# A small bias table in DRAM read as overlapping rows, and a second one spread out in 16 pieces

## The reference, cut to what matters

```python
dist = pos_b[None, :, None] - idx
bias = jnp.moveaxis(rel_bias[t5_bucket(dist)], -1, 2)      # first block: 32 buckets x 16 heads
...
drow = rs + jnp.arange(win_r) - r + WIN_ROWS - 1
bias = jnp.transpose(rpb[:, drow][:, :, dcol], (0, 2, 3, 1, 4))   # second block: 8 heads x 15 x 31
```

## Time and profile before

| | us |
|---|---|
| median of 3 runs | 914.88 |
| lowest and highest | 914.59, 915.59 |
| the profiled execution, its own time | 912.87 |
| span of the profile | 911.1 |

### The profile page before, as it was taken

How to read it: one execution, slowest core, us unless ns; L and a number is a source line. 1 busy time by engine, 2 the same in 40 slices (tenths; PEclk the granted TensorE clock), 3 DMA queues, 4 the chain that set the end, 5 groups by cost and what they waited for, 6 DMA issues and landing times.

```text
span 911.1 us, 17577 instructions
## 1 busy us (share of the span) xinstructions
PE 893.8 (98%) x7192; PEld 869.4 (95%) x7192; DVE 656.3 (72%) x1261; ACT 499.7 (55%) x907; POOL 46.6 (5%) x62
## 2 busy tenths in 40 slices
PE   8999987999999999999999999999999999999998
PEld 7988987999999898899999999999999999999998
DVE  6878626988877695575667555566798788887873
ACT  5695827774435556667768444434545454445551
POOL 0000000000000125200000000021020000000000
PEclk9999997999999999999999999999999999999999
DMA  9918799978877743048545655526445222465541
GB/s 307 313 47 279 142 185 355 305 252 277 293 252 232 246 137 126 2 149 264 181 148 194 205 169 185 189 78 177 161 150 184 93 71 70 140 208 164 180 144 47
DMA packets 164753, 166.30 MB, mean 183 GB/s; under 512 B 16672, under 2 KB 161216, under 8 KB 164416
## 3 DMA queue, kind: packets, MB, share of 16 engines
q1 hardware_dynamic: 164672, 165.17, 57.7%
HBM read 162.01 MB, written 4.98 MB: 183 GB/s over the span
## 4 chain that ended last, share of the span: by engine, by line
PE 83%; DMA 5%; DVE 4%; ACT 3%; SPq 3%; issue 2%; POOL 0%; DVEq 0%; ACTq 0%
PE ps L304 21%; PE ps L306 21%; PE ps L308 21%; DMA e_scratch<-eb 3%; PE ps L1505 2%; PE ps L1503 2%; PE ps L1507 2%; PE ps L1562 2%; PE ps L1076 1%; DVE wl L271 1%; PE ps L1597 1%; PE ps L1599 1%; PE ps L1601 1%; SPq L2174 1%; DMA raw<-in_rec_w_in_dram 1%
## 5 line engine op out<-in xcount | busy, mean ns | idle before, releaser
L304 PE MATMUL ps<-xh,wh 128*128 128x256 f32 x1136 | 326.9, 288 | 8.9 <-ACT tmp L798 8.9
L271 DVE TENSOR_TENSOR wl<-raw,wh 128x1024 fp32r<-128x1024 f32 x256 | 308.5, 1221 | 31.7 <-ACT wh L264 31.5
L306 PE MATMUL ps<-xl,wh 128*128 128x256 f32 x1136 | 322.2, 284 | 0.0
L308 PE MATMUL ps<-xh,wl 128*128 128x256 f32 x1136 | 322.1, 284 | 0.0
L264 ACT ACTIVATE wh<-raw 128x1024 fp32r<-128x1024 f32 x256 | 266.5, 1050 | 94.0 <-PE ps L308 69.2
L304 PEld LDWEIGHTS ps<-xh,wh 128*128 128x128 f32 x1136 | 218.4, 192 | 12.0 <-ACT tmp L798 9.1
L306 PEld LDWEIGHTS ps<-xl,wh 128*128 128x128 f32 x1136 | 218.5, 192 | 0.3
L308 PEld LDWEIGHTS ps<-xh,wl 128*128 128x128 f32 x1136 | 218.4, 192 | 0.0
L304 PE MATMUL ps<-hh,wh 128*128 128x256 f32 x512 | 143.2, 280 | 0.0
L306 PE MATMUL ps<-hl,wh 128*128 128x256 f32 x512 | 143.2, 280 | 0.0
L308 PE MATMUL ps<-hh,wl 128*128 128x256 f32 x512 | 143.2, 280 | 0.0
(11 more groups left out here) (359 smaller groups left out, 1458.2 us busy)
## 6 DMA issues: line engine op xcount, KB each, us to landing
raw<-in_w_in_dram SPq DMA_DIRECT2D x34, 1024.0 KB, 5.2
raw<-in_mlp_up_dram SPq DMA_DIRECT2D x32, 1024.0 KB, 6.2
raw<-in_mlp_down_dram SPq DMA_DIRECT2D x32, 1024.0 KB, 6.0
aw<-in_w_adaT_dram SPq DMA_DIRECT2D x24, 512.0 KB, 5.4
raw<-in_rec_w_in_dram SPq DMA_DIRECT2D x7, 1024.0 KB, 10.9
raw<-in_att_w_in_dram SPq DMA_DIRECT2D x6, 1024.0 KB, 6.2
raw<-in_rec_w_out_dram SPq DMA_DIRECT2D x4, 1024.0 KB, 6.4
raw<-in_att_w_o_dram SPq DMA_DIRECT2D x4, 1024.0 KB, 5.0
```

Of the source, the lines that this page charges most:

```text
L271: e.tensor_tensor(parts_of(i)[1], raw_of(i), f32(parts_of(i)[0]), op=ALU.subtract).then_inc(S["wl"], 1)
L304: e.matmul(o, H[:, first + n], xh[:, k], start=start and n == 0, stop=False)
L306: e.matmul(o, H[:, first + n], xl[:, k], start=False, stop=False)
L308: ins = e.matmul(o, L[:, first + n], xh[:, k], start=False, stop=stop and n == len(ks) - 1)
```

## The change

EB is copied from PSUM with its columns in reverse, and `e_scratch` keeps just the 16 rows of 384 values. BT is then loaded as rows that overlap in the source: partition p reads 256 values of each head from column 1 + p on. GpSimd reads BT backwards. The spreading of `rpb` is taken away from where it was and issued in 16 copies of 7 x 64 rows, one behind each of chunks 66 to 81; the semaphore is waited for at 256 instead of 16.

```diff
+    def backwards(ap):
+        (_, n), step = ap.ap[1], ap.ap[1][0]
+        return bass.AP(ap.tensor, ap.offset + (n - 1) * step, [ap.ap[0], [-step, n]])
...
-    e_dram = nc.dram_tensor("e_scratch", (16, 128, 256), F32, kind="Internal").ap()
+    e_dram = nc.dram_tensor("e_scratch", (16, 384), F32, kind="Internal").ap()
...
-        e.activation(EB[:], ps["eb"], ACT.Copy).then_inc(S["eb"], 1)
+        e.activation(EB[:], backwards(ps["eb"]), ACT.Copy).then_inc(S["eb"], 1)
...
-            e.tensor_tensor(BM[h % 2][:, 0:128], BT[:, h, 128:256], MK[:, 0:128], op=ALU.add).then_inc(S["bm"], 1)
-            e.tensor_tensor(BM[h % 2][:, 128:384], BT[:, h], MK[:, 128:384], op=ALU.add).then_inc(S["bm"], 1)
+            e.tensor_tensor(BM[h % 2][:, 0:128], backwards(BT[:, h, 0:128]), MK[:, 0:128], op=ALU.add).then_inc(
+                S["bm"], 1)
+            e.tensor_tensor(BM[h % 2][:, 128:384], backwards(BT[:, h]), MK[:, 128:384], op=ALU.add).then_inc(
+                S["bm"], 1)
...
-        e.dma_start(e_dram[:], bass.AP(eb.tensor, eb.offset + 127, [eb.ap[0], [-1, 128], [1, 256]])).then_inc(
-            S["e"], 16)
-        e.dma_start(w_dram[4:116], bass.AP(rpb.tensor, 4 * 31 + 15, [[31, 112], [-1, 64], [1, 64]])).then_inc(
-            S["w"], 16)
+        e.dma_start(e_dram[:], EB[:]).then_inc(S["e"], 16)
         q.wait_ge(S["e"], 16)
...
-                e.dma_start(BT[:], e_dram.rearrange("h p c -> p h c")).then_inc(S["bt"], 16)
+                e.dma_start(BT[:], bass.AP(e_dram.tensor, 1, [[1, 128], [384, 16], [1, 256]])).then_inc(S["bt"], 16)
...
-                q.wait_ge(S["w"], 16)
+                q.wait_ge(S["w"], 256)
...
             sync_chunk(e, q, c)
+            if 66 <= c < 82:
+                r = 4 + 7 * (c - 66)
+                e.dma_start(w_dram[r:r + 7], bass.AP(rpb.tensor, r * 31 + 15, [[31, 7], [-1, 64], [1, 64]])).then_inc(
+                    S["w"], 16)
```

More of the change, by code:

```diff
@@ L2205, in sync_all @@
         sync_chunks(e, q, 16, 19)
-        eb = EB[:]
         q.wait_ge(S["eb"], 1)
-        e.dma_start(e_dram[:], bass.AP(eb.tensor, eb.offset + 127, [eb.ap[0], [-1, 128], [1, 256]])).then_inc(
-            S["e"], 16)
-        e.dma_start(w_dram[4:116], bass.AP(rpb.tensor, 4 * 31 + 15, [[31, 112], [-1, 64], [1, 64]])).then_inc(
-            S["w"], 16)
+        e.dma_start(e_dram[:], EB[:]).then_inc(S["e"], 16)
         q.wait_ge(S["e"], 16)
```

## The result

| | before | after |
|---|---|---|
| median, us | 914.79 (914.59 to 915.59, 4 runs) | 902.54 (901.83 to 902.86, 4 runs) |
| the profiled execution, its own time | 912.87 | 902.53 |
| span of the profile | 911.1 | 900.7 |

The ratio is 0.9863, 95% interval 0.9846 to 0.9881: 12.3 us less in the medians, 10.3 in the two profiled executions. The forecast was 903.7, 1.2 too high, with a range of 902.5 to 905.5. The measured median lies on its lower end, and by the ratio (0.9863 x 914.88 = 902.3) the time is just under it. The direction and the mechanism held; the gain that I had forecast, 11.2 us, was short by a tenth.

What follows compares the result with a forecast made beforehand. TensorE bounds the kernel, busy 98% of the span; its stall waiting for chunk 19 goes whole, all other parts cost 0: 914.88 - 11.2 = 903.7 us, range 902.5 to 905.5.

Steps and rivals of the forecast that it cites:

- What bounds, and the chain: First perceptron, 132 to 146 us: e_scratch's write, then w_scratch's drain, delay upward weight chunk 19; ScalarE, then TensorE wait.
- The stall's price, 11.2 us: TensorE's stall from 132.11 to 145.92 us, 13.8 less 2.6, slow clock included; all of it goes.
- The small write, 2 us: Write of e_scratch as 16 rows, 24 KB, taken to land in 2 us, bounds 1.7 to 9.3.
- The cushion of 9 us: First perceptron: TensorE loses time only some 9 us after ScalarE starts waiting; 17.9 of wait made 8.95 of idle.
- B: Attention: reading BT backwards costs GpSimd half more, 0.6 us a head; time 903.9, chance 0.05.
- C: Attention: reading BT backwards costs GpSimd double, 1.2 us a head; time about 907, chance 0.04.
- E: GpSimd becomes the attention's bound; slower from 2.5 times today's cost, about 926 at three times; chance 0.03.
- Rival D: Small e_scratch write nearly as slow as the large; TensorE loses 2 to 3 us, time about 906, chance 0.04.
- I carry the same difference to it: In the sum: the median's 2.0 us above the profiled execution is kept for the changed kernel, 914.88 - 11.2 = 903.7.
- The pieces at 0: Sixteen rpb copies at 440 to 530 us or a little before: 0.4 to 0.7 us issue each, costing 0.
- the seven-engine estimate, 0.9 us a piece: If a piece of 7 rows runs on seven DMA engines only: 14.4 us in all, share from 0.57 to 0.73.
- The 19 us of spare: Around chunk 73: 24 us from issue to its high part, less about 5 for landing; covers the pieces' delay.

Runs made afterwards that it cites:

- e2: Kernel before with only the spreading of rpb moved to the 16 places, the 2 MB write of e_scratch kept: 907.93 us, ratio 0.9935.
- e3: Kernel after with the copy to w_scratch in one piece at its old place, behind the small write: 902.53 us, ratio 0.9869.
- e8: Kernel after with the copy to w_scratch in one piece at its old place, plus one further such copy that nobody reads: 902.46 us.
- e9: Kernel after with the copy to w_scratch in one piece at its old place, plus two further such copies that nobody reads: 907.87 us.
- e6: Kernel before with the 2048 rows of e_scratch written from a tile of 128 partitions, replacing the bias: 902.92 us in a single execution.

## Why the prediction was right or wrong

**What bounds, and the chain**: right. The idle time, ScalarE's wait and chunk 19 vanish together, and `e2`, `e3`, `e8` and `e9` move them by the steps of the chain.

**The stall's price, 11.2 us**: right for the execution that was profiled (11.1 by the marks). That the whole of it goes held as well.

**The small write, 2 us**: 1.5. **Chunk 19 landed by 112**: it was issued at 103.87, and ScalarE never waited for it.

**The cushion of 9 us**: right, 9.0 in `e9`.

**BT's load at 11 us, GpSimd as now, VectorE no worse**: right, 10.8, 0.46 and 0.72, and 16.51 of 20. Rivals B, C and E, which rest on GpSimd, fall. Rival D, that the small write is nearly as slow as the large, falls with 1.5 us; its guess that the time lay in the source partitions fits `e6`, and its price, 2 to 3 us lost if 24 us stay, was low: `e2` lost 5.4, 3.6 of idle and 1.8 of slow clock, which I had left out.

**The sum: the step that failed is "I carry the same difference to it", with the stall's price of one execution, 11.2 us, as its term.** The profiled execution of before was 2.0 us below its median, and I took this for something that the changed kernel would share. It does not: its profiled execution (902.53) lies on its median (902.54). What was to be subtracted from the median was the loss of a median run, and 914.79 - 902.54 = 12.3 is what went. What varies from run to run is the stall: 8.8 to 11.5 us in the six profiles, with nothing behind the mark to vary with it, and by the clocks more than that in the longer runs, up to 918.4. So "the stall's size is known to 0.3", on which the range rested, held for one execution and not for the runs. Of the 2.0 us at least 1.2 belonged to the stall and went with it, by 12.3 - 11.1; the other 0.8 is what the start of the kernel after came later than in the profile of before, and a median run of before may have started later too. That the stall of a run at 914.8 is this long was not seen in a trace; it was seen at 912, where loss and gain agree. All three runs of before (914.59 to 915.59) lay above the profiled one, which was the sign to read. The size and sign of the miss are in part luck: where before took 912.0 the same subtraction, 11.2, would have been 1 to 2 us too much.

**The pieces at 0**: right in the result, wrong in size. I put a piece at 0.4 to 0.7 us of issue, by a sixteenth of the whole. It takes 0.77 to issue in an idle queue and 2.5 to 3.7 in a busy one, so with three behind each chunk a chunk came only every 10 us, and the kernel took 45 us more. On the engines the seven-engine estimate, 0.9 us a piece, was near: a piece alone held the share at 0.46 for a microsecond. The 19 us of spare stand against a rate, not against one delay, and a rate adds up over sixteen chunks.

## What to carry to other kernels

The stall that the change took away was also what made the runs of the kernel before spread, within a set of runs and from one set to another. Where the profiled execution lies below the median, price the stall for the median run, or profile until one comes near it. The 2 MB write from 16 SBUF partitions was three times as slow as one from 128; here it was enough to write each value once and let the load read overlapping rows of DRAM, which cost that load nothing. When a transfer is cut into pieces, give each piece a slowest dimension of 16, and test the spare by doubling and tripling it.

## What the runs showed of the hardware that was not expected

- 2 MB in rows of 1 KB took 24.4 us from 16 partitions, at a DMA share of 0.81 and 94 GB/s, and 8.1 us from 128, in another order of the rows in DRAM; aligning the rows changed it by 0.5.
- A copy of 1.8 MB from DRAM to DRAM behind that write landed 33.0 us after its issue in two profiles and 30.6 to 31.2 in four, and before's time went with it from set to set.
- After an idle of 7.2 to 7.5 us TensorE ran at clock 0.50 for 13, 23 or 26 matmuls in three executions of one kernel (loss less idle: 1.5, 2.5 and 2.7 us).
- Spread over DRAM three times over, 1.8 MB of 256-byte rows in pieces of 7 x 64 rows left the DMA share at 0.58, with SyncE issuing without a gap; in pieces of 16 x 64 rows it was 0.85. A piece of 7 alone ran at a share of 0.44 to 0.46, one of 16 at 0.86.
- An issue on SyncE took 0.77 us with an idle queue and 2.5 to 3.7 us with a busy one, for the same piece.
